# Squared MLP blocks turned by VectorE and placed through DRAM, in place of TensorE transposes

## The reference, cut to what matters

```
u = _rmsnorm(h, norm_mlp_g)
a = einsum('bsd,df->bsf', u, w_up)        # 2048 -> 8192
a = square(relu(a))
h = h + einsum('bsf,fd->bsd', a, w_down)  # 8192 -> 2048
```

## Time and profile before

| | us |
|---|---|
| median of 3 runs | 2290.82 |
| lowest, highest | 2287.92, 2291.16 |
| profiled execution, span from first to last instruction | 2285.8 |
| TensorE busy | 2266.4 (99%) |
| VectorE busy | 1556.3 (68%) |
| ScalarE busy | 1109.7 (49%) |

### The profile page before, as it was taken

The page is one execution under the profiler, slowest core; times in us unless marked ns, Lnnn a source line. Parts: engine busy times, 40 slices in busy tenths (PEclk is TensorE's granted clock), DMA queues, the critical chain, the costliest instruction groups (busy, mean ns, idle before and its releaser), DMA issues.

```text
span 2285.8 us, 28964 instructions
## 1 busy us (share of the span) xinstructions
PE 2266.4 (99%) x10345; PEld 1864.5 (82%) x10345; DVE 1556.3 (68%) x1869; ACT 1109.7 (49%) x1531; POOL 223.5 (10%) x361
## 2 busy tenths in 40 slices
PE   9999999999999999999999999999999999999998
PEld 7888888888888888888878877787888888888886
DVE  7886778778867877887767664556555545555556
ACT  6446455555545545545463463545444344444444
POOL 0121001111111111110011000000210011100110
PEclk9999999999999999999999999999999999999999
DMA  8983679978888888886677664564665666656663
GB/s 311 331 272 97 206 235 320 317 267 293 275 281 287 273 301 269 272 280 215 220 242 245 209 203 129 186 220 158 210 203 194 207 207 198 207 185 201 195 195 126
DMA packets 250005, 528.12 MB, mean 231 GB/s; under 512 B 22144, under 2 KB 22544, under 8 KB 248592
## 3 DMA queue, kind: packets, MB, share of 16 engines
q1 hardware_dynamic: 214256, 405.32, 54.2%
q0 software_dynamic: 33664, 116.17, 14.8%
q10 hardware_dynamic: 1952, 4.85, 0.6%
HBM read 517.87 MB, written 4.21 MB: 228 GB/s over the span
## 4 chain that ended last, share of the span: by engine, by line
PE 97%; DVE 1%; ACT 1%; DMA 0%; issue 0%; SPq 0%; ACTq 0%; DVEq 0%; POOLq 0%
PE acc L1798 30%; PE acc L1807 29%; PE acc L1802 29%; PE tp L1869 2%; PE m L1880 1%; PE acc L1820 0%; PE acc L1825 0%; PE acc L1830 0%; PE tp L2206 0%; PE tp L2224 0%; PE tp L2218 0%; PE acc L2000 0%; PE tp L2131 0%; PE acc L1853 0%; PE acc L1851 0%
## 5 line engine op out<-in xcount | busy, mean ns | idle before, releaser
L1090 DVE TENSOR_TENSOR wlo<-wring,whi 128x1024 fp32r<-128x1024 f32 x762 | 919.5, 1216 | 562.6 <-ACT whi L565 455.4
L565 ACT ACTIVATE whi<-wring 128x1024 fp32r<-128x1024 f32 (+1 forms) x510 | 532.1, 1047 | 720.4 <-PE acc L1807 719.3
L1798 PE MATMUL acc<-whi,xhi 128*128 128x512 f32 x2056 | 558.5, 393 | 0.1
L1802 PE MATMUL acc<-whi,xlo 128*128 128x512 f32 x2056 | 550.0, 389 | 0.0
L1807 PE MATMUL acc<-wlo,xhi 128*128 128x512 f32 x2056 | 549.9, 389 | 0.0
L1802 PEld LDWEIGHTS acc<-whi,xlo 128*128 128x128 f32 x2056 | 386.0, 188 | 81.1
L1807 PEld LDWEIGHTS acc<-wlo,xhi 128*128 128x128 f32 x2056 | 386.0, 188 | 80.7
L1798 PEld LDWEIGHTS acc<-whi,xhi 128*128 128x128 f32 x2056 | 381.2, 188 | 86.3 <-issue 9.0
L575 ACT ACTIVATE whi<-wring 128x1024 fp32r<-128x1024 f32 x266 | 280.8, 1059 | 319.8 <-PE acc L1807 318.1
L1120 DVE SCALAR_TENSOR_TENSOR macc<-mring,csil,macc 128x512 f32<-128x512 f32 x480 | 344.0, 747 | 29.3 <-DMA mring<-w_mod 23.0
L460 POOL DMA_DIRECT2D mring<-w_mod x192 | 138.9, 724 | 1047.4 <-DVE macc L1120 998.9
(11 more groups left out here) (277 smaller groups left out, 1313.7 us busy)
## 6 DMA issues: line engine op xcount, KB each, us to landing
wring<-w_up SPq DMA_DIRECT2D x216, 512.0 KB, 4.7
wring<-w_down SPq DMA_DIRECT2D x216, 512.0 KB, 5.1
mring<-w_mod POOLq DMA_DIRECT2D x192, 512.0 KB, 5.3
wring<-w_in SPq DMA_DIRECT2D x184, 512.0 KB, 5.2
wring<-w_gate SPq DMA_DIRECT2D x88, 512.0 KB, 4.3
wring<-w_out SPq DMA_DIRECT2D x64, 512.0 KB, 4.9
tmpT<-blk POOLq DMA_DIRECT2D x128, 32.0 KB, 3.4
gbig<-ctx_in POOLq DMA_DIRECT2D x2, 1024.0 KB, 8.1
```

Of the source, the lines that this page charges most:

```text
L565: act.activation(whi[:, piece_slot(c, piece), 0:half], wring[:, g4, piece * half:(piece + 1) * half], ACT.Copy).then_inc(hi_done, 1)
L1090: dve.tensor_tensor(wlo[:, h4, 0:half], wring[:, g4, piece * half:(piece + 1) * half], whi[:, h4, 0:half].bitcast(F32), ALU.subtract).then ...
L1798: pe.matmul(acc[:, 2 * pair + t, :], hi[:, tile, t * P:(t + 1) * P], whi[:, h4, w], start=(tile == starts), stop=False)
L1802: pe.matmul(acc[:, 2 * pair + t, :], lo[:, tile, t * P:(t + 1) * P], whi[:, h4, w], start=False, stop=False)
```

## The change

For blocks 0, 1 and 2 of each chunk the TensorE transposes go. Instead:

- VectorE, at g = 5, 9 and 13, transposes 32x32 squares of `blk` into `blk2` (`turn_relu`).
- SyncE stores `blk2` (512 KB) to a DRAM tensor, then issues one more weight load, waits until the store is complete, and issues four loads of 128 KB that set the strips on their partitions (`tmpT`).
- ScalarE rounds the result in four instructions (`round_relu`) and VectorE subtracts in four (`remain_relu`), at g = 9 (block 0), g = 13 (block 1) and g = 17 (block 2).
- Block 3 is turned by TensorE as before, at g = 17.
- TensorE waits for the remainders of blocks 0 and 1 before g = 16, and for those of block 2 before g = 18.
- Relu writes to `blk` (before: to `blk2`) and waits for the turn of the block before.

The diff, cut to its core:

```diff
 # SyncE
+            def store_strips():
+                sp.wait_ge(relu_turned, c.at("rs", T, T))
+                sp.dma_start(strip_rows.rearrange("i b j n -> (i b) j n"), strips).then_inc(strips_stored, 16)
+            def place_strips():
+                sp.wait_ge(strips_stored, c.at("rs", 16, 16))
                 for j in range(4):
+                    sp.dma_start(placed[32 * j:32 * j + 32, :, :], strip_rows[:, :, j, :].rearrange("i b n -> b i n"))\
+                        .then_inc(relu_moved, 16)
+            def up_block(i, j):
+                for kg in range(KT // KG):
+                    load(v[kg, :, :, bass.ds(i * D + j * NB, NB)])
+                    if j >= 2 and kg == 2:
+                        store_strips()
+                    if j >= 2 and kg == 3:
+                        place_strips()
...
+                        if n == 0 and kg == 2:
+                            store_strips()
+                        if n == 0 and kg == 3:
+                            place_strips()
 # ScalarE
+                if j:
+                    act.wait_ge(relu_turned, c.at("rt", T, T))
...
+            def round_relu(tile):
+                act.wait_ge(relu_moved, c.at("rm", RELU_MOVES, RELU_MOVES))
+                for k in range(KG):
+                    act.activation(xhi[:, tile + k, :]..., moved[:, k], ACT.Copy).then_inc(relu_hi, 1)
...
-                    if 1 <= j <= 4:
-                        round_banks(xhi, 4 * (j - 1), 2)
+                    if 2 <= j <= 4:
+                        round_relu(4 * (j - 2))
+                    if j == 4:
+                        round_banks(xhi, 12, 2)
 # VectorE
+            def turn_relu():
+                dve.wait_ge(blk_ready, c.at("blk", 1))
+                dve.wait_ge(relu_moved, c.at("rt", 0, RELU_MOVES))
+                for t in range(T):
+                    dve.transpose(turned[:, t], blk[:, t, :]...).then_inc(relu_turned, 1)
+            def remain_relu(tile):
+                for k in range(KG):
+                    dve.wait_ge(relu_hi, c.at("rk", 1))
+                    dve.tensor_tensor(xlo[:, tile + k, :]..., moved[:, k], xhi[:, tile + k, :]..., ALU.subtract).then_inc(relu_lo, 1)
...
                     if g % 4 == 1 and 1 <= j <= 4:
-                        remain_banks(xhi, xlo, 4 * (j - 1), 2)
+                        if j >= 2:
+                            remain_relu(4 * (j - 2))
+                        if j < 4:
+                            turn_relu()
+                        if j == 4:
+                            remain_banks(xhi, xlo, 12, 2)
 # TensorE
                     for kg in range(3):
+                        if j == 4 and kg in (0, 2):
+                            pe.wait_ge(relu_lo, c.at("rs", KG * (2 if kg == 0 else 3), KG))
                         multiply(hi, lo, (kg,), 4, pair)
-                        if kg == 1 and 1 <= j <= 4:
+                        if kg == 1 and j == 4:
                             pe.wait_ge(blk_ready, c.at("blk", j))
                             turn_rows(blk, 2)
```

More of the change, by code:

```diff
@@ L55 @@
 WARM = 4
-X_HI = 2 * (2 * KG - 1) + 4 * KG + 8 * MLP_CHUNKS + 2 * KG + 2 * KG + 8
+MLP_MOVED = 3
+X_HI = 2 * (2 * KG - 1) + 4 * KG + 2 * MLP_CHUNKS + 2 * KG + 2 * KG + 8
 H0 = 2
@@ L254, in two_blocks @@
             sem(n) for n in ("squares_turned", "rows_moved", "moved_hi", "moved_lo"))
+        relu_turned, strips_stored, relu_moved, relu_hi, relu_lo = (
+            sem(n) for n in ("relu_turned", "strips_stored", "relu_moved", "relu_hi", "relu_lo"))
         out_s = sem("out_s")
@@ L366, in two_blocks @@
         BANKS = {"z": 1, "suffix": 1, "ctx_state": 1, "state": 2, "turn": 1, "out": 1, "conv": 2}
-        T_O = 8 + 8 + 8 * MLP_CHUNKS + 8 + 8 + 4 + BANKS["out"] + sum(
+        T_O = 8 + 8 + 2 * MLP_CHUNKS + 8 + 8 + 4 + BANKS["out"] + sum(
             BANKS.get(step[0], 0) for steps in BESIDE[1].values() for step in steps)
@@ L372, in two_blocks @@
         MOVES = 16 * 16
+        RELU_MOVES = 4 * 16
         block = ctx.enter_context(nc.Block())
@@ L405, in _ @@
                     block_of(w_out, i * (2 * NB) + j * NB)
-            with c.loop(sp, MLP_CHUNKS, g=32) as i:
-                for j in range(4):
-                    block_of(w_up, i * D + j * NB)
-                for n in range(4):
-                    block_of(w_down, n * NB, kg0=i * 4)
+            def store_strips():
[3 more added lines that the diff above has]
+                sp.wait_ge(strips_stored, c.at("rs", 16, 16))
+                for j in range(4):
+                    sp.dma_start(placed[32 * j:32 * j + 32, :, :], strip_rows[:, :, j, :].rearrange("i b n -> b i n"))\
+                        .then_inc(relu_moved, 16)
+                c.add("rs")
+            def up_block(i, j):
+                v = w_up.rearrange("(g k p) n -> g p k n", k=KG, p=P)
+                for kg in range(KT // KG):
[4 more added lines that the diff above has]
+                        place_strips()
+            with c.loop(sp, MLP_CHUNKS, g=32, rs=MLP_MOVED) as i:
+                for j in range(4):
+                    up_block(i, j)
+                for n in range(4):
+                    v = w_down.rearrange("(g k p) n -> g p k n", k=KG, p=P)
+                    for kg in range(KG):
+                        load(v[bass.ds(i * 4 + kg, 1), :, :, n * NB:(n + 1) * NB].rearrange("a p k n -> (a p) k n"))
+                        if n == 0 and kg == 2:
+                            store_strips()
+                        if n == 0 and kg == 3:
+                            place_strips()
             for names in (C_IN, X_IN):
@@ L821, in relu_square @@
                     act.wait_ge(rstd_done, 2)
+                if j:
+                    act.wait_ge(relu_turned, c.at("rt", T, T))
+                    c.add("rt")
                 for t in range(T):
-                    last = act.activation(blk2[:, t, :], acc[:, 2 * (j % 2) + t, :], ACT.Relu, scale=rstd[:, 1, t:t + 1])
+                    last = act.activation(blk[:, t, :], acc[:, 2 * (j % 2) + t, :], ACT.Relu, scale=rstd[:, 1, t:t + 1])
                 last.then_inc(blk_half, 1)
@@ L826, in relu_square @@
                 act.wait_ge(blk_half, c.at("half"))
-                act.activation(blk[:, :, :], blk2[:, :, :], ACT.Square).then_inc(blk_ready, 1)
+                act.activation(blk[:, :, :], blk[:, :, :], ACT.Square).then_inc(blk_ready, 1)
                 c.add("blk")
+            def round_relu(tile):
+                act.wait_ge(relu_moved, c.at("rm", RELU_MOVES, RELU_MOVES))
+                for k in range(KG):
+                    act.activation(xhi[:, tile + k, :].rearrange("p (t i b) -> p t i b", t=T, i=4),
+                                   moved[:, k], ACT.Copy).then_inc(relu_hi, 1)
+                c.add("rm")
             def square_block(n, first):
@@ L866, in _ @@
             root_and_scale(2, u_g, u_g)
-            with c.loop(act, MLP_CHUNKS - 1, 1, g=32, q=8, half=4, blk=4, ha=4, ssq=4 * T, mt=5):
+            with c.loop(act, MLP_CHUNKS - 1, 1, g=32, q=2, half=4, blk=4, ha=4, ssq=4 * T, mt=5, rt=MLP_MOVED, rm=MLP_MOVED):
                 mlp_chunk()
@@ L1381, in set_gain1 @@
                 dve.wait_ge(gain_set, 2)
+            def turn_relu():
+                dve.wait_ge(blk_ready, c.at("blk", 1))
+                dve.wait_ge(relu_moved, c.at("rt", 0, RELU_MOVES))
+                for t in range(T):
+                    dve.transpose(turned[:, t], blk[:, t, :].rearrange("p (k j b) -> p k j b", k=KG, j=4)).then_inc(relu_turned, 1)
+                c.add("rt")
+            def remain_relu(tile):
+                for k in range(KG):
+                    dve.wait_ge(relu_hi, c.at("rk", 1))
+                    dve.tensor_tensor(xlo[:, tile + k, :].rearrange("p (t i b) -> p t i b", t=T, i=4), moved[:, k],
+                                      xhi[:, tile + k, :].bitcast(F32).rearrange("p (t i b) -> p t i b", t=T, i=4),
+                                      ALU.subtract).then_inc(relu_lo, 1)
+                    c.add("rk")
             def mlp_chunk(i, first=False, last=False):
@@ L1393, in mlp_chunk @@
                     if g % 4 == 1 and 1 <= j <= 4:
-                        remain_banks(xhi, xlo, 4 * (j - 1), 2)
+                        if j >= 2:
+                            remain_relu(4 * (j - 2))
+                        if j < 4:
+                            turn_relu()
+                        c.add("blk")
+                        if j == 4:
+                            remain_banks(xhi, xlo, 12, 2)
                     if g in MLP_REDUCED and not (last and g == 30):
@@ L1419, in _ @@
             norm_scale(2, u_g, u_g)
-            with c.loop(dve, MLP_CHUNKS - 1, 1, g=32, q=8, hi=8, m=32, ma=80, mt=5, msum=5 * KG) as i:
+            with c.loop(dve, MLP_CHUNKS - 1, 1, g=32, q=2, hi=2, m=32, ma=80, mt=5, msum=5 * KG, blk=4, rt=MLP_MOVED,
+                        rk=KG * MLP_MOVED) as i:
                 mlp_chunk(i)
@@ L2093, in mlp_chunk @@
                 c.add("blk", 4)
```

(3 more changed lines are left out.)

1 line of the change is left out of this document (added).

## The result

The change makes the kernel slower: 2325.04 us (median of 4 runs, 2324.61 to 2326.44) against 2290.8, a ratio of 1.0155 with a 95% interval of 1.0143 to 1.0167. The profiled execution's span is 2323.5 us, 37.7 more than before. I had forecast 2301 in a range of 2292 to 2314.

What follows compares the result with a forecast made beforehand. TensorE, 97% of the chain, was taken as the bound. Per chunk -2.70 + 2.32 + 3.13 = +2.75, four times +11.0, less 0.96: +10.0 on 2290.8, forecast as 2301 us, range 2292 to 2314.

Steps and rivals of the forecast that it cites:

- the two places: TensorE was to wait in each chunk after g = 15, 2.32 us, and before g = 18, 3.13 us.
- What a turn gives: Each block that TensorE no longer transposes was to save it 0.90 us, 2.70 us a chunk, 10.8 over four chunks.
- VectorE's string: VectorE back to back from g = 9 through g = 14, 738.17 to 770.64, making TensorE wait 2.32 us after g = 15.
- The wait before g = 18: TensorE was to wait 3.13 us per chunk for VectorE's four remainders of block 2, released late at g = 17.
- The wait after g = 15: TensorE was to wait 2.32 us per chunk for VectorE's last SC1 step, delayed by the moved blocks' work.
- rival (d): `w_mod` or the strips land late, 1 to 2 us a chunk more: 2305 to 2309 us; chance 15%.
- about 7 us between a slot's release and its use: Time the SC1 steps' `w_mod` loads have, against a median 5.3 us; store and four loads may add 1 or 2.
- Rival (c): The clock falls at the new waits, 2.26 us a fall: 2310 us at g = 18 only, 2319 at both; chance 15%.
- The last chunk's credit: The existing 0.96 us wait after g = 22 in the last chunk was to go, as TensorE reaches g = 18 later.
- my case: Both new TensorE waits come, after g = 15 and before g = 18: 10.0 us slower, 2301 us; chance 50%.
- SyncE's detour: SyncE's store, four loads and waits for a moved block take some 10 us, 15 at most, hidden from TensorE.
- The sign that VectorE has no idle time from g = 9 to g = 14: In the changed trace VectorE was to run without idle time from g = 9 to g = 14.

Runs made afterwards that it cites:

- The two smaller versions: Against the kernel before: block 0 alone moved, 2287.34 us, ratio 0.9988; blocks 0 and 1 moved, SC1 summed after g = 16, GT1 after g = 23, 2283.53 us, ratio 0.9977.

## Why the prediction was wrong, step by step

- **The sign and the two places** were right: both waits came where I put them. The one before g = 18 came from the cause that I gave, the one after g = 15 from that cause for half of its length only.
- **What a turn gives**: 0.90 us. The two smaller versions gain 1.6 of 3.6 and 5.4 of 7.2 us, and their intervals just hold the full gain, so these runs neither confirm the 0.90 closely nor speak against it.
- **VectorE's string**: forecast 2.32 us. Without the traffic it is 2.09 to 2.15. The arithmetic held to 0.1 us in 32.
- **The wait before g = 18**: forecast 3.13, measured 3.21, 2.87, 2.87 and 2.93.
- **The wait after g = 15 was mis-sized: 9.3 us in the sum, 16.6 measured.** I priced late `w_mod` loads as rival (d), 1 to 2 us a chunk at 15%. They are a consequence of the moved blocks and cost 2 us on average (16.6 - 8.5 over four chunks), 3.15 in chunk 1, above my bound. The step "about 7 us between a slot's release and its use" against a *median* landing of 5.3 left 1.7 us of slack, and I had just added 1 MB in this very stretch.
- **The clock failed, and it is the largest miss: the sum has no term for it, and 16.3 to 17.9 us were lost.** Rival (c), at 15%, came in full: eight falls. I took 2.26 us a fall from the FFN's opening; here the pair in a chunk costs about 4.1 us, 16.3 in four. So the size of a fall was about right and its chance was not. Rows 10 should have been read the other way round: idle times of 1.49 and 0.57 us had been enough there, and I forecast 2.3 and 3.1. And the row that I held against it, the attention at a clock of 1.00, was one execution's: after the change the same code, untouched, ran at 0.54.
- **The last chunk's credit** of 0.96 us did not come: its wait after g = 22 grew to 1.62. On the way to that sum VectorE waited 3.28 us for a `w_mod` load (before: 1.62).
- **The sum**: -10.8 + 9.3 + 12.5 - 1.0 = +10.0 forecast; -10.8 + 16.6 + 11.9 + 1.1 + 17.0 + 1.9 = +37.7 measured. The 1.9 arises ahead of the MLP, in code that the change leaves as it was. (c) and (d) were listed as alternatives to my case, while they are additions to it: my case creates the idle time that (c) needs. A range that adds them, up to 2301 + 18 + 8, would have held the time.
- **SyncE's detour** cost TensorE no wait for a weight, as forecast. That the strips of block 2 come in time for g = 17 was right too: ScalarE waited for strips in no chunk of the changed kernel, nor in the one with SC1 summed later, where TensorE did not stand idle after g = 15. They are late for g = 16 only.
- **The sign that VectorE has no idle time from g = 9 to g = 14** did not come: 1.3 to 3.1 us a chunk, for `w_mod`.

## What to carry to other kernels

On a kernel bound by TensorE, ask of each helper's work when its result is due, not how busy the helper is: 0.28 us of slack at one sum decided here, on an engine 68% busy. When a forecast contains a new idle time of TensorE as long as those here, price the fall of the clock with it, as a term and not as a rival: every wait of 2.8 us or more in these traces had one, and some of about two. And move a deadline together with those behind it, or the wait turns up at the next one.

## What the runs showed of the hardware

- In the MLPs of all these traces, each of the 27 waits of TensorE of 2.8 us or more brought the granted clock to 0.50. Of nine waits between 1.9 and 2.6 us four did (1.90, 2.07, 2.14, 2.32) and five did not (2.09, 2.09, 2.15, 2.48, 2.51). Of the shorter ones none did. So in this middle range the length of a wait alone does not tell.
- A fall cost 1.4 to 2.9 us of matmuls behind the wait (eight falls, 16.3 us). The same code in the attention had a fall in one profiled execution and none in another.
- Filling idle time with 27 unused matmuls a chunk made the changed kernel 14.7 us faster.
- 1 MB of added store and load traffic per moved block went with 512 KB loads on another queue that were up to 3.1 us late for their reader in the dual stretch; with an eighth of the bytes none was.
